# Sampled sparse attention: the squares of keys and their sums taken three halves ahead instead of two, with a third buffer

## What is computed

```python
ks = rms_norm(rows[:, :, 2], g_k[1])      # keys of 2048 past positions, from the paged cache
vs = rows[:, :, 3]
s = einsum(q, gathered ks) * scale + bias; p = masked_softmax(s, valid); o_sel = einsum(p, gathered vs)
kw = rms_norm(win_k, g_k[2])              # the same over a window of 512 keys
o = gt[:, :, 0] * o_cmp + gt[:, :, 1] * o_sel + gt[:, :, 2] * o_win

def rms_norm(x, g):
    y = xf * lax.rsqrt(jnp.mean(xf * xf, axis=-1, keepdims=True) + EPS)
```

## Time and profile before

| | us |
|---|---|
| median of 3 runs | 3523.07 |
| lowest, highest | 3521.96, 3527.87 |
| the profiled execution | 3520.66 |
| its span in the trace | 3518.8 |
| the sampled stage in it, from its first product to the last product with the values | about 838.5 to 1079 |
| TensorE busy, share of the span | 3194.0, 91% |

### The profile page before, as it was taken

One profiled execution on the slowest core, in us unless ns is written; L12 is line 12 of the kernel. 1 busy time (PEld: TensorE's weight loads), 2 busy tenths in 40 slices (PEclk: granted clock), 3 DMA queues, 4 the chain that ended last, 5 costly groups with the idle time before them and its releaser, 6 DMA issues. The chain is left out here.

```text
span 3518.8 us, 56593 instructions
## 1 busy us (share of the span) xinstructions
PE 3194.0 (91%) x23855; PEld 2984.5 (85%) x23855; DVE 1583.9 (45%) x1660; ACT 1285.2 (37%) x1320; POOL 201.2 (6%) x137
## 2 busy tenths in 40 slices
PE   7799999975678999999999999956789999999999
PEld 5699999843347999999999999944289999999999
DVE  4543444336554544434443354344654443344433
ACT  3432345324563443333332342245134333233322
POOL 0000001002430000000000000023300000000000
PEclk9899999968888999999999999967789999999999
DMA  4545444333654455555555545301644555555553
GB/s 154 177 157 190 138 153 139 112 115 101 211 168 141 147 161 162 167 168 168 162 163 167 169 145 166 119 32 62 225 170 144 164 162 164 168 168 164 162 165 135
DMA packets 317268, 537.10 MB, mean 153 GB/s; under 512 B 18245, under 2 KB 115519, under 8 KB 316104
## 3 DMA queue, kind: packets, MB, share of 16 engines
q1 hardware_dynamic: 316440, 529.73, 46.3%
q10 hardware_dynamic: 624, 4.46, 0.3%
HBM read 517.23 MB, written 25.19 MB: 154 GB/s over the span
## 5 line engine op out<-in xcount | busy, mean ns | idle before, releaser
L509 DVE TENSOR_TENSOR project_weights_low<-ring,project_weights_high 128x2048 fp32r<-128x2048 f32 x344 | 788.4, 2292 | 1207.0 <-ACT project_weights_high L441 1207.0
L441 ACT ACTIVATE project_weights_high<-ring 128x2048 fp32r<-128x2048 f32 x344 | 658.7, 1915 | 1256.9 <-PE project_banks L369 1256.7
L367 PE MATMUL project_banks<-high,project_weights_high 128*128 128x288 f32 x2560 | 761.9, 298 | 31.1 <-DVE project_weights_low L499 27.3
L368 PE MATMUL project_banks<-low,project_weights_high 128*128 128x288 f32 x2560 | 760.1, 297 | 0.0
L369 PE MATMUL project_banks<-high,project_weights_low 128*128 128x288 f32 x2560 | 759.9, 297 | 0.0
L367 PE MATMUL project_banks<-up_high,project_weights_high 128*128 128x288 f32 x2048 | 605.4, 296 | 0.0
L368 PE MATMUL project_banks<-up_low,project_weights_high 128*128 128x288 f32 x2048 | 605.2, 296 | 0.0
L369 PE MATMUL project_banks<-up_high,project_weights_low 128*128 128x288 f32 x2048 | 605.1, 295 | 0.0
L367 PEld LDWEIGHTS project_banks<-high,project_weights_high 128*128 128x128 f32 x2560 | 486.9, 190 | 32.8 <-DVE project_weights_low L499 28.0
L368 PEld LDWEIGHTS project_banks<-low,project_weights_high 128*128 128x128 f32 x2560 | 486.6, 190 | 0.0
L369 PEld LDWEIGHTS project_banks<-high,project_weights_low 128*128 128x128 f32 x2560 | 485.3, 190 | 0.0
(11 more groups left out here) (510 smaller groups left out, 3032.4 us busy)
## 6 DMA issues: line engine op xcount, KB each, us to landing
ring<-in_w_up_dram SPq DMA_DIRECT2D x128, 1024.0 KB, 5.2
ring<-in_w_down_dram SPq DMA_DIRECT2D x128, 1024.0 KB, 5.1
ring<-in_gla_w_in_dram SPq DMA_DIRECT2D x40, 1024.0 KB, 5.0
h<-in_cache_nsa_kv_dram SPq DMA_DIRECT2D x256, 128.0 KB, 2.3
ring<-in_w_out_dram SPq DMA_DIRECT2D x32, 1024.0 KB, 5.2
ring<-in_nsa_w_in_dram SPq DMA_DIRECT2D x28, 1024.0 KB, 5.1
sp_keys_values<-in_cache_nsa_kv_dram SPq DMA_DIRECT2D x80, 256.0 KB, 3.8
ring<-in_w_mem_kv_dram SPq DMA_DIRECT2D x16, 1024.0 KB, 6.3
```

The lines of the kernel that those rows point to most:

```text
L367: nc.tensor.matmul(bank, w_high, moving_high[:, kt], start=(kt == 0), stop=False)
L368: nc.tensor.matmul(bank, w_high, moving_low[:, kt], start=False, stop=False)
L441: nc.scalar.activation(weights_high[:, c % 2], g.ring[:, c % RING], ACT.Copy).then_inc(rounded, 1)
L509: nc.vector.tensor_tensor(weights_low[:, c % 2], g.ring[:, c % RING], weights_high[:, c % 2].bitcast(F32), ALU.subtract).then_inc(split, 1)
```

## The change

A third buffer of squares is added, in the first 1024 columns of `cmp_k`, the tile of the compressed keys. Squares and sums are taken at k+3 instead of k+2, and `all_keys` begins one step earlier on every engine. square(n) waits for the sum of n-2 instead of n-1 (`wait(act, k_mean, ...)` means that many sums are done, so n-2 is: sum(n-3) is done). square(2), the first that overwrites `cmp_k`, waits for the products that read it (`small_scored`). No instruction is added or removed.

```diff
-        squares = [g.mem_k[0][:].rearrange("p h k -> p (h k)"), g.mem_v[0][:].rearrange("p t n -> p (t n)")]
+        squares = [g.mem_k[0][:].rearrange("p h k -> p (h k)"), g.mem_v[0][:].rearrange("p t n -> p (t n)"),
+                   g.cmp_k[:, 0:CHUNK_PAGES * GROUPS * HD]]
...
-        def ticks(first=-2, last=TOTAL + 1):
+        def ticks(first=-3, last=TOTAL + 1):
...
             def square(n):
                 act.wait_ge(loaded[n % V_SLOTS], loaded_by(n))
-
-                wait(act, k_mean, n - 1)
-                nc.scalar.activation(squares[n % 2], keys[n].rearrange("p q n -> p (q n)"), ACT.Square
+                if n == 2:
+                    act.wait_ge(small_scored, 1)
+                wait(act, k_mean, n - 2)
+                nc.scalar.activation(squares[n % 3], keys[n].rearrange("p q n -> p (q n)"), ACT.Square
...
-                    if in_range(k + 2):
-                        square(k + 2)
+                    if in_range(k + 3):
+                        square(k + 3)
...
-                linked(nc.vector.tensor_reduce(ss[:, n], squares[n % 2].rearrange("p (c d) -> p c d", d=HD),
+                linked(nc.vector.tensor_reduce(ss[:, n], squares[n % 3].rearrange("p (c d) -> p c d", d=HD),
...
-                    if in_range(k + 2):
-                        sum_squares(k + 2)
+                    if in_range(k + 3):
+                        sum_squares(k + 3)
```

## The result

The changed kernel takes **3532.37 us** (median of 20 runs, 3526.87 to 3536.99), the kernel before 3523.08 beside it (20 runs, 3519.16 to 3529.58): ratio **1.0025**, 95% interval 1.0018 to 1.0032. It is slower by 9.3 us, where the forecast was 4.3 slower. Its profiled span is 3528.5.

The account below looks back on a forecast made before the run. Chains of waits, not a full engine, were taken to bound the kernel. Gains in steady steps and pair ends against losses at the front and late loads summed to +4.25 us: 3527.4, range 3520 to 3531 (8 in 10: 3516 to 3536).

Parts of the forecast that it names:

- Bound and steady steps: Chains of waits set the time; ACT's root wait for the sum falls from 62.6 us to under 20.
- plain double steps: Two steps between inverses away from pair ends: 7.2 to 7.3 us apart, 0.4 gained for each.
- Those with the window's COPY: Double steps at the end of a pair, 9.16 and 9.10 us before: taken as 7.7, 1.5 gained each.
- load(10) and the late COPY: First pair: load(10) holds its square, the COPY then meets a scaling, and I(10) comes 2.2 us later.
- The scaling that holds a sum's second instruction: On DVE, the sum's TENSOR_SCALAR waits until the scaling is over, 2.2 us after I(k).
- The front: Stage start: sum(1) and sum(2) delay the part at -0.9 by 4.9 us; the first exponential's stretch nets +2.0.
- The exponential behind the last take: Pair end: negated maximum stands behind a sum; exponential at I(12)+2.8 instead of 3.88, 1.1 us gained a pair.
- n = 34: Load(34), just before the third exponential, holds its square: 1.2 us lost in the third pair.
- The stall: Squares 16, 26 and 36: ACT waits 3.7 us for the DMA, and I(16) comes 3.8 later.
- The sum: Four stretches at +2.0, +0.3, +0.85 and +1.1, nothing outside them: together +4.25 us.
- The slower one: Idle PE drops its clock from 2.4 to 1.2 GHz; eight slow double steps, priced at 8 us: 3535, chance 0.20.
- The sign set for it: Prediction wrong if PE's clock in the stage, 0.78 to 0.93 by stretch, changes by more than 0.05.

Follow-up runs that it names:

- experiment 2: Kernel before, with squares and sums of halves 1, 2 and 3 one step earlier, nothing else: 3529.6 us, ratio 1.0015.
- experiment 3: Changed kernel with halves 0 to 4 two ahead as before, three ahead from half 5 on: 3532.84 us, ratio 1.0023.
- experiment 8: Changed kernel with 24 identity transposes on PE ahead of the products of set 3 in the first three pairs: 3527.85 us, ratio 1.0010.
- experiment 5: Changed kernel with halves up to 4, and halves 6, 7 and 8 of each later pair, two ahead: 3524.13 us, ratio 1.0002.

## Why the prediction was half right

- **Bound and steady steps: right.** Root's wait for the sum is gone from the list (62.6 before), and the plain double steps are 7.12 to 7.36 (the first two by inverses at 881.49, 888.62, 895.74; forecast 7.2 to 7.3). Those with the window's COPY are 7.25, 7.25 and 8.08 (forecast 7.7), those with the fourth chunk's 8.62 and 8.51 in the second and third pairs. The first pair's, with load(10) and the late COPY, was worked out as 7.45 and 2.2 and is 9.64. The scaling that holds a sum's second instruction is there too, in six sums of 0.65 to 0.88 against 0.17.
- **The front: right as a size, wrong as a term.** The part at -0.9 began at 856.59, 4.6 later counted from the stage's start (4.9 forecast), and the first exponential 1.5 later (2.0). Added to the kernel before (experiment 2) it costs 5.2 by the medians; taken out of the changed kernel (experiment 3) it gives nothing: in its trace 2.8 of the 4.8 us are gone by I(6), to that experiment's own double step and to a slow turn(4). So it cannot be treated as a term that adds up with the others, and its share in the 9.3 stays open.
- **The exponential behind the last take: wrong in two pairs of three.** It was to come 2.8 behind I(12), I(22) and I(32) instead of 3.88, a gain of 1.1 each. It came 3.96, 2.55 and 3.89 behind. In the first and third pairs the sum ahead of the negated maximum waited for a square whose load was late, square(14) by 1.86 and square(34) by 1.42. The forecast had n = 34 as late, but the loads of 11 and 14, held to be early enough, stopped their squares for 1.51 and 1.86. That the first stretch still came near its forecast is in part luck: I(4) was 4.0 later, not 4.8, and the double steps behind it gave 0.9 us more than forecast.
- **The stall: right in place and size, wrong in what hangs on it.** The forecast was 3.7 us of waiting at squares 16, 26 and 36; the trace has 3.09, 3.36 and 4.00. The step that failed is "3.8 later than before ... From there to the exponential I give back 0.5 ...". Counted from the issue of load(16), I(15) came 3.7 later (8.48 against 4.76), but I(16) 5.5 (15.80 against 10.29), not 3.8, and I(18) 5.1 (23.16 against 18.10), not 3.3. The forecast put the clock at nothing: turn(14) of 937.67 took 1.92 instead of 1.04, and the scores behind it were slow too. With the clock held (experiment 8) I(16) came 3.95 later, as forecast. The wait of 3 to 4 us on ACT is one of 3 to 4 us on PE, and the first turn behind it ran at half clock. In the last pair I(36) came 6.7 later in after and 3.8 in experiment 8; 0.9 of this difference is the load that landed sooner.

  SP was left out too, with less effect here: load(18) needs turn(14), which stands on PE behind the products that wait for ACT's copies. So the stall holds back a later load. SP's timeline of after, loads 16, 17 and 18; load(18) stood at 934.34 before:

```profile
928.10 2.40 SPq L1842 DMA_DIRECT2D ring<-in_cache_nsa_kv_dram  x4
932.12 2.66 SPq L1842 DMA_DIRECT2D sp_keys_values<-in_cache_nsa_kv_dram  x4
939.62 0.93 SPq L1846 DMA_DIRECT2D sp_keys_values<-in_state_nsa_win_dram  x2
```

  Squares 18 and 19 waited only 0.22 and 0.62 for these late loads in after. Their lateness shows when something ahead of them gets faster: in experiment 8 square(19) waited 1.72 and took back what the clock had given. In the third and last pairs loads 28 and 38 were not held back.
- **The sum.** The stretches were forecast at +2.0, +0.3, +0.85 and +1.1 and came at +1.5, +1.3, +1.2 and +4.2, with +1.1 behind the last exponential, where nothing was expected. The last pair's is the term that was mis-sized most. By experiment 8 I estimate 1 to 2 us of its 4.2 as PE's clock (1.1 at the exponential, 1.9 at I(36)); one trace cannot give it closer. The last products were 1.1 longer because the lower clock lasted longer: the third set's transposes took 1.12 instead of 0.90. In the ten traces without the 52 transposes the stretch is 16.8 to 17.2 where that set was faster than 1.0, and 17.7 to 18.3 where it took 1.12. What makes the clock come back sooner or later there stays open, and experiment 5, not slower than before, has the long stretch too (17.7). The forecast's own addition is 0.1 off: the median before and 4.25 make 3527.3, not 3527.4.
- **The rivals.** The slower one named the right mechanism, but as an alternative to the forecast, not as a consequence of its stall. It asked for two slow double steps per pair; one slow turn behind each stall was enough for a part of its price. Both happened together. The result lies between the two, above the 3520 to 3531 that the forecast gave itself and inside the wider 3516 to 3536, near its upper end, in the class (above 3530.1) that had a chance of 0.28. The sign set for it, a clock changed by more than 0.05 in a stretch, did not show (the last pair's fell from 0.93 to 0.89): a mean over 30 us hides 6 us at half clock. The rule of the Trainium skill's page "DMA: Bandwidth & Descriptors" (section "Anatomy of one DMA") would give an estimate of 2.8 for each wait instead of 3.7. All three waits are longer than that, and load(16) landed in a median of 3.5 as before.

## What to carry to other kernels

Before a step is moved ahead on an in-order engine, look for every place where its input cannot be early, and move it everywhere else: the same lookahead cost 9 us with three such places in it and gained 3 without them, the front and the late loads. A stall is charged with what is queued behind it on every engine that it reaches, and with the clock of a TensorE that it leaves idle. What a faster engine gives back counts only up to the next load that cannot come earlier, as square(19) showed in experiment 8. And an experiment that undoes one part must be read for what its own edit adds: the table of experiment 3 put two sums ahead of one inverse.

## What the runs showed of the hardware

In the changed kernel 3.00 us of idle PE in the second pair were followed by a turn of 1.92 us instead of 1.04, and 4.08 us in the last pair by 6 us at the lower clock (0.50 from 1043 to 1049). 24 transposes in that idle time, 2.78 us of work on otherwise unused output, kept the granted clock at 1.00. Idle work of 16, 16, 16 and 52 transposes behind the exponentials made the kernel before 8.5 us faster without any change to what it computes, more than the 3.2 that the best order of squares gained. Beside a scaling on POOL a 128x8 TENSOR_SCALAR on DVE took 0.65 to 0.88 us instead of 0.17. The four DMAs of load(16) landed in a median of 2.0 us with 64 KB each and of 3.5 with 256 KB.
